# Alternating the two maps' score matmuls of differential attention on the two partition halves, in phases of 512 keys

## What is computed

```python
def diff_attention(q, k, v, lam, lam_init, g_sub, slopes):
    for i in range(S // Q_BLOCK):                       # Q_BLOCK = 128
        kend = q0 + Q_BLOCK
        s = einsum('bqhmd,bkhmd->bhmqk', q[:, q0:kend], k[:, :kend]) * scale
        s = where(allowed, s - slopes * dist, NEG)
        p = softmax(s, axis=-1)
        a = p[:, :, 0] - lam * p[:, :, 1]
        outs.append(einsum('bhqk,bkhe->bqhe', a, v[:, :kend]))
    o = rmsnorm(concatenate(outs, axis=1), g_sub) * (1.0 - lam_init)
```

## Time and profile before

| what | value |
|---|---|
| median of 3 runs | 2858.18 us |
| lowest and highest run | 2855.99 and 2860.78 us |
| span of the profiled execution | 2860.5 us |
| TensorE matmul busy | 2731.5 us, 95% |
| VectorE busy | 1237.1 us, 43% |
| ScalarE busy | 962.7 us, 34% |
| mean granted TensorE clock | 0.961 of full speed |
| share of L1223 (all scores) in the chain that ended last | 5% |

### The profile page before, as it was taken

The page is one execution under the profiler, slowest core; times in us unless marked ns, Lnnn a source line. Parts: engine busy times, 40 slices in busy tenths (PEclk is TensorE's granted clock), DMA queues, the critical chain, the costliest instruction groups (busy, mean ns, idle before and its releaser), DMA issues.

```text
span 2860.5 us, 36998 instructions
## 1 busy us (share of the span) xinstructions
PE 2731.5 (95%) x12825; PEld 2215.9 (77%) x12825; DVE 1237.1 (43%) x2444; ACT 962.7 (34%) x1696; POOL 116.6 (4%) x59
## 2 busy tenths in 40 slices
PE   6999999979999999999989999998899999999998
PEld 5777777768888888888877777776788888888886
DVE  5565664654322322223436666556443222232234
ACT  4344454553321212112334444545423122121223
POOL 3000010001100000000200000000020000000001
PEclk8999998969999999999999999988799999999998
DMA  4100100003111111111130100000211111111112
GB/s 151 30 23 23 29 16 16 16 8 103 44 52 44 51 52 44 51 44 51 44 104 18 28 22 22 16 23 9 74 52 44 52 44 52 44 51 51 44 48 77
DMA packets 214404, 126.40 MB, mean 44 GB/s; under 512 B 14702, under 2 KB 213400, under 8 KB 213528
## 3 DMA queue, kind: packets, MB, share of 16 engines
q1 hardware_dynamic: 214296, 125.09, 14.7%
HBM read 112.49 MB, written 12.58 MB: 44 GB/s over the span
## 4 chain that ended last, share of the span: by engine, by line
PE 85%; DVE 6%; issue 4%; ACT 3%; DVEq 1%; ACTq 0%; DMA 0%; SPq 0%; POOL 0%; POOLq 0%
PE ps L1124 54%; PE ps L1171 18%; PE ps L1223 5%; PE ps L1253 3%; PE ps L1235 2%; PE ps L1255 1%; DVE probs L915 1%; PE ps L1130 1%; ACT probs L615 1%; DVEq L918 1%; PE ps L1193 1%; DVE part L861 1%; PE ps L1365 1%; DVE neg_max L923 1%; DVE part L858 1%
## 5 line engine op out<-in xcount | busy, mean ns | idle before, releaser
L1124 PE MATMUL ps<-h_hi,w_hi 128*128 128x512 f32 x1024 | 315.6, 389 | 0.0
L1124 PE MATMUL ps<-h_lo,w_hi 128*128 128x512 f32 x1024 | 315.3, 389 | 0.0
L1035 DVE TENSOR_TENSOR xt<-ps,xt 128x1024 f32 (+1 forms) x80 | 98.0, 1225 | 502.4 <-PE ps L1124 501.0
L1124 PE MATMUL ps<-u_hi,w_lo 128*128 128x512 f32 x1024 | 315.2, 389 | 0.0
L1124 PE MATMUL ps<-u_hi,w_hi 128*128 128x512 f32 x1024 | 315.2, 389 | 0.0
L1124 PE MATMUL ps<-h_hi,w_lo 128*128 128x512 f32 x1024 | 315.2, 389 | 0.0
L1124 PE MATMUL ps<-u_lo,w_hi 128*128 128x512 f32 x1024 | 315.2, 389 | 0.0
L481 ACT ACTIVATE w_hi<-w_raw 128x1024 fp32r<-128x1024 f32 x144 | 151.2, 1050 | 453.3 <-PE ps L1124 450.7
L1171 PE MATMUL ps<-h_hi,w_hi 128*128 128x512 f32 x736 | 266.7, 444 | 36.1 <-DVE w_lo L846 14.4
L1171 PE MATMUL ps<-h_lo,w_hi 128*128 128x512 f32 x736 | 237.9, 405 | 0.0
L1171 PE MATMUL ps<-h_hi,w_lo 128*128 128x512 f32 x736 | 236.3, 403 | 0.0
(11 more groups left out here) (152 smaller groups left out, 4046.1 us busy)
## 6 DMA issues: line engine op xcount, KB each, us to landing
w_raw<-in_w_up_dram SPq DMA_DIRECT2D x128, 256.0 KB, 3.1
w_raw<-in_w_down_dram SPq DMA_DIRECT2D x128, 256.0 KB, 3.0
w_raw<-in_w_in_dram SPq DMA_DIRECT2D x92, 256.0 KB, 3.2
x_saved<-xt SPq DMA_DIRECT2D x2, 4096.0 KB, 12.9
w_raw<-in_w_out_dram SPq DMA_DIRECT2D x32, 256.0 KB, 3.0
xt<-x_saved SPq DMA_DIRECT2D x4, 2048.0 KB, 7.4
rows<-in_x_dram SPq DMA_DIRECT2D x4, 1024.0 KB, 9.1
out_dram<-rows SPq DMA_DIRECT2D x4, 1024.0 KB, 5.8
```

The lines of the kernel that those rows point to most:

```text
L1035: V.tensor_tensor(xt[:, 2 * m + j], r, xt[:, 2 * m + j], ALU.add).then_inc(evacuated, 1)
L1124: mm = nc.tensor.matmul(ps[j][:, bass.ts(t, BANK)], w[:, j, c], h[:, c, bass.ts(t, BANK)], start=(c == 0 and n == 0), stop=(c == NC - 1 an ...
```

## The change

Both maps' scores of a step are now made together in a phase of up to 512 keys: pass by pass, map 0 on its half of the partitions into bank 0 of `ps[0]`, map 1 on the other half into bank 1. A step of up to 512 keys (i = 0 to 3) has one phase, at the place where map 0's scores stood. A wider step (i = 4 to 7) has a second one for the keys beyond 512, at the place where map 1's scores stood. On VectorE `pair_max` follows the same phases: it reads both banks, writes the maxima of the second phase to a new tile `far_max`, and makes `neg_max` of both maps only after the last phase. The second phase's scores wait until the first has been read. ScalarE's program is unchanged. The number of score passes, their columns and their weight loads are unchanged too.

```diff
--- before.py
+++ after.py
@@ -255,6 +255,7 @@
         eps = small("eps", [P, 1])
         rms_col = small("rms_col", [P, NQ])
         row_max = small("row_max", [P, 8])
+        far_max = small("far_max", [P, 8])
         neg_max = small("neg_max", [P, 8])
         row_sum = small("row_sum", [P, 8])
         sink_exp = small("sink_exp", [P, 8])
@@ -924,6 +925,35 @@
                                             sink[:, bass.ds(sink_at, 1)], neg, ALU.max, ALU.mult)
                     e.then_inc(max_done, 1)
 
+                def pair_max(s0, m0, t, n, key0, width, sc):
+
+                    wide = width > BANK
+                    k1 = min(width, key0 + BANK)
+                    dve.wait_ge(scored, m0 + (n + (1 if wide and key0 == 0 else 2)))
+                    dve.wait_ge(turned, s0 + (t - 1 + CREDIT))
+                    V.memset(wait_slot[:], 0.0)
+                    to = far_max if key0 else row_max
+                    for k in range(2):
+                        at = (n + k) % 8
+                        e = V.tensor_tensor_reduce(out=probs[:, (n + k) % 4, key0:k1],
+                                                   in0=ps[0][:, BANK * k:BANK * k + k1 - key0],
+                                                   in1=far[:, S - width + key0:S - width + k1], scale=1.0, scalar=-3e38,
+                                                   op0=ALU.add, op1=ALU.max, accum_out=to[:, at:at + 1])
+                        if k or not wide:
+                            e.then_inc(scores_read, 1)
+                    if k1 < width:
+                        return
+                    V.drain()
+                    for k in range(2):
+                        at = (n + k) % 8
+                        neg = neg_slope[:, bass.ds(sc + k, 1)]
+                        if wide:
+                            e = V.tensor_scalar(neg_max[:, at:at + 1], row_max[:, at:at + 1], far_max[:, at:at + 1], neg,
+                                                ALU.max, ALU.mult)
+                        else:
+                            e = V.tensor_scalar(neg_max[:, at:at + 1], row_max[:, at:at + 1], neg, None, ALU.mult)
+                        e.then_inc(max_done, 1)
+
                 def combine(m0, n, width):
 
                     dve.wait_ge(exp_done, m0 + (n + 2))
@@ -965,7 +995,8 @@
                             width = window(grp, i)[1] * P
                             n = run.map0[t] + k
                             if grp == "A":
-                                biased_max(s0, m0, t, 1, n, width, far[:, S - width:S], 2 * pair0 + (2 * pp + k))
+                                if k * BANK < width:
+                                    pair_max(s0, m0, t, run.map0[t], k * BANK, width, 2 * pair0 + 2 * pp)
                             elif grp == "B":
                                 at = 2 * (pair0 + pp) + k
                                 biased_max(s0, m0, t, 1, n, width, near[:, 2 * P - width:2 * P], at,
@@ -1225,6 +1256,17 @@
                                                   start=(p == 0), stop=(p == 2))
                     mm.then_inc(scored, 1)
 
+                def pair_scores(m0, n, qs, ks, i, key0, width):
+
+                    k1 = min(width, key0 + BANK)
+                    pe.wait_ge(scores_read, m0 + (n + (1 if key0 else 0) + CREDIT))
+                    for p, (q, k) in enumerate(((q_hi, k_hi), (q_hi, k_lo), (q_lo, k_hi))):
+                        for j in range(2):
+                            half = slice(j * HD, (j + 1) * HD)
+                            mm = nc.tensor.matmul(ps[0][:, BANK * j:BANK * j + k1 - key0], q[half, qs, i * P:(i + 1) * P],
+                                                  k[half, ks, key0:k1], start=(p == 0), stop=(p == 2))
+                    mm.then_inc(scored, 1 if width > BANK else 2)
+
                 def turn_probs(s0, t, slots, b0, blocks, early, ready, count):
                     pe.wait_ge(ready, count)
 
@@ -1268,6 +1310,10 @@
                             pe.wait_ge(split_done, NPART * l + slab0 + (3 if grp == "B" and pp == 2 else 3 * pp - 2))
 
                         n = run.map0[t]
+                        if grp == "A":
+                            if k * BANK < blocks * P:
+                                pair_scores(m0, n, (run.parity + pp) % 2, kv_slot(grp, pp), i, k * BANK, blocks * P)
+                            return
                         p0, read = (BANK * k, n) if grp == "B" else (0, n + k)
                         scores(m0, n + k, (run.parity + pp) % 2, kv_slot(grp, pp), i, k if j is None else j, k0,
                                blocks * P, p0, read)
```

## The result

| what | before | after |
|---|---|---|
| median | 2858.85 us (6 runs) | 2879.96 us (6 runs) |
| lowest and highest run | 2855.99 and 2868.91 | 2870.12 and 2888.83 |
| ratio of after to before, 95% interval | | 1.0072 [1.0056, 1.0088] |
| profiled execution, span | 2860.5 us | 2870.9 us |
| mean granted clock in the profiled execution | 0.961 | 0.957 |

The change costs 21 us. Its direction is that of the forecast and the median lies in its range, near the low end, but the size is half of the 44 us.

What follows compares the result with a forecast made beforehand. TensorE was taken to bound the kernel before, a VectorE-ScalarE chain the wide steps after. The terms summed to +11.0 us a call, +44 for four calls, on 2858.2: 2902 us, 8 in 10 from 2877 to 2932.

Steps and rivals of the forecast that it cites:

- What TensorE saves: Score passes of both maps overlap and narrow steps lose a group each: 65 us if TensorE stayed the bound.
- full overlap at 512 columns: Two maps' score passes of 512 columns on different halves take the time of one; assumed, shown only for 256.
- The chain in the wide steps: Steps 4 to 7: late `neg_max` makes VectorE and ScalarE take turns; 29.4 us, +3.8 and +6.1 in the two heads.
- Steps 0 to 4 of the first head: Narrow steps at a call's start: TensorE's saving less waits for `pt_lo` and the combination, net -2.2 us a call.
- Border and end: Step 7 into the next head, +1.3 us with that head's narrow steps; step 15 to the last turn, +2.0.
- The clock, a rival at 15%: TensorE's clock falls after its new stands, 8 falls costing up to 24 us; result 2905 to 2930; 15%.
- That TensorE stays the bound: Rival: the exponentials catch up and TensorE's saving counts in full, faster by 65 us, 2793; 6%.
- That pairs of 512 don't overlap: Rival: wide score passes gain nothing from pairing, costing 2.4 us a call more, 2912; 9%.
- That the chain costs only what is saved: Rival: each forecast VectorE-ScalarE chain is too long by a fifth; result 2845 to 2875; 12%.
- The rule of the Trainium skill: Row tiling speeds the array but not PSUM evacuation; by that sentence, little or none of the 65 us gain.

Runs made afterwards that it cites:

- x8_first: Kernel before, with both maps' scores paired only in each head's first step (i = 0, 128 keys); 2852.30 us.
- x12_pieces: Changed kernel, with both projection pieces of a wide step put ahead of the values on TensorE, none between second phase and turn; 2877.85 us.
- x1_narrow: Changed kernel, with pairing kept only in steps of up to 512 keys; wider steps go map by map as before; 2833.52 us.
- x14_head0_7: Kernel before, plus pairs in narrow steps and in steps 4 to 6 of a call's first head, those with ScalarE's splits and store ahead of the first exponential; 2828.54 us.
- x5_late_neg: Kernel before, scores map by map; in wide steps only map 0's `neg_max` is made later, after map 1's maximum; 2926.11 us.
- x2_act_order: Changed kernel, with the part's high split and `store_o` moved ahead of the first exponential on ScalarE in wide steps; 2843.94 us.

## Why the forecast was right in sign and wrong in size

**What TensorE saves: right.** The step I was least sure of, full overlap at 512 columns, holds (0.90 us for six passes). The scores' own busy time in layer 0, 288 passes each, before and after:

```profile
95.00:376.00 281.00, 69.05 (x288) 46.22 (x288) 0.98 0.09 23
95.00:384.00 289.00, 40.98 (x288) 23.46 (x288) 0.93 0.08 22
```

That is 28 us less, some 56 in both layers, where the forecast had 65. TensorE's busy time as a whole fell by only 32.6 us, because the values' passes were longer (in layer 0 L1253 and L1255 together 65.0 us before, L1295 and L1297 together 77.2 after) and the turns too. That goes with the lower granted clock of the calls (0.93 against 0.98); how much of it the clock makes isn't separated.

**The chain in the wide steps: right in kind, too long by 1.0 and 1.9 us a stretch.** The forecast's step 5 to 6 was 11.5 us. The changed kernel, VectorE and ScalarE:

```profile
136.44 0.42 DVE L938 CUSTOM_DVE_ANT_0 probs<-ps,far 128x256 f32<-128x256 f32 x1
...
137.31 0.46 DVE L951 TENSOR_SCALAR neg_max<-row_max,far_max,neg_slope 128x1 f32<-128x1 f32 x2
137.62 1.03 ACT L616 ACTIVATE probs<-probs,neg_max,slope_now 128x768 f32<-128x768 f32 x1 [4.79 <-DVE neg_max L951]
...
138.65 1.04 ACT L519 ACTIVATE k_hi<-part 128x1024 fp32r<-128x1024 f32 x1
...
140.19 1.02 ACT L616 ACTIVATE probs<-probs,neg_max,slope_now 128x768 f32<-128x768 f32 x1
...
141.21 1.04 ACT L514 ACTIVATE w_hi<-w_raw 128x1024 fp32r<-128x1024 f32 x1
...
142.28 1.23 DVE L847 TENSOR_TENSOR w_lo<-w_raw,w_hi 128x1024 fp32r<-128x1024 f32 x1 [1.33 <-ACT w_hi L514]
...
143.43 0.68 DVE L901 TENSOR_TENSOR pt_lo<-ps,pt_hi 128x512 fp32r<-128x512 f32 x1
...
144.16 0.38 PE L1295 MATMUL ps<-v_parts,pt_hi 128*128 128x256 f32 x1 [2.68 <-DVE pt_lo L901]
144.23 0.69 DVE L938 CUSTOM_DVE_ANT_0 probs<-ps,far 128x512 f32<-128x512 f32 x1
...
144.84 0.69 DVE L938 CUSTOM_DVE_ANT_0 probs<-ps,far 128x512 f32<-128x512 f32 x1
...
146.04 1.02 DVE L966 SCALAR_TENSOR_TENSOR probs<-probs,lam_ratio 128x768 f32<-128x768 f32 x1
146.98 0.42 DVE L984 TENSOR_REDUCE ps<-ps 128x128 f32<-128x256 f32 x1
147.32 0.55 DVE L938 CUSTOM_DVE_ANT_0 probs<-ps,far 128x384 f32<-128x384 f32 x1
```

Read down, this is the chain of the forecast, link for link, and from 136.44 to 147.32 it takes 10.88 us. From start to start the links are: to the exponential 1.18 (forecast 1.28), two exponentials 2.05 (2.06), `k_hi` and `store_o` 1.54 (1.64), `w_hi` up to `w_lo` 1.07 (1.00), `w_lo` 1.15 (1.15), `pt_lo` 0.80 (0.88), two maxima 1.22 (1.50), up to the combination 0.59 (0.60), combination 0.94 (0.94), reduction 0.34 (0.43). The mis-sized terms are those for which I added durations. Neighbours on one engine start before the one ahead has ended: the two maxima of 512 keys start 0.61 us apart at 0.69 us each, where I had put a gap of 0.07 between them. Step by step the first head has 7.5, 10.9 and 9.1 us (forecast 8.2, 11.5, 9.7). That makes the wide terms 27.5 and 28.4 and not 29.4: 1.9 and 1.0 us a call, 12 of the 28 us by which the sum of the terms (44 us) missed the calls' 15.7.

**Steps 0 to 4 of the first head: the term that failed.** The forecast had -2.2 us, of it 0.7 for step 0; measured is -6.4, which is 17 of the 28 us. I had priced the pair there by TensorE's passes alone and put what the old order cost at a call's start at nothing: a wait of map 1's scores, and the low clock behind it. Rows 1 showed the place, TensorE idle for half of 236 to 242.2, and I put it to the border and took it as given. The timeline of before shows what part of that idle time was:

```profile
236.50 0.33 PE L1223 MATMUL ps<-k_hi,q_hi 64*128 64x128 f32 x1
...
242.27 0.29 DVE L915 CUSTOM_DVE_ANT_0 probs<-ps,far 128x128 f32<-128x128 f32 x1
...
242.63 0.33 PE L1223 MATMUL ps<-k_hi,q_hi 64*128 64x128 f32 x1 [2.75 <-DVE row_max L915]
...
249.00 0.38 PE L1223 MATMUL ps<-k_hi,q_hi 64*128 64x256 f32 x1
```

At the start of the second call, map 1's scores wait 2.75 us for VectorE to read map 0's, with three pieces of projection queued behind them; and the stretch right behind has the low clock, 0.67 in rows 1. After:

```profile
241.76 0.33 PE L1266 MATMUL ps<-k_hi,q_hi 64*128 64x128 f32 x2
...
247.58 0.29 DVE L938 CUSTOM_DVE_ANT_0 probs<-ps,far 128x128 f32<-128x128 f32 x1
...
249.13 0.39 PE L1266 MATMUL ps<-k_hi,q_hi 64*128 64x256 f32 x2
```

Map 1's scores have their own bank and don't wait, so the pieces run meanwhile, and the granted clock of 242.0 to 245.6 us is 1.00. From step 0's scores to step 1's it is 7.4 us instead of 12.5. The fourth call has the same wait (2.76 us before, none after), and in these two calls the whole stretch shrinks by 7.5 us.

The first and third call don't have this wait, before or after, and still shrink by 5.9 and 4.5 us. Their granted clock from the first maximum to step 4 rises from 0.87 and 0.95 to 0.95 and 1.00; in all four calls of before it was below full, in the changed kernel in the first alone. What the score passes bring there and what the clock gives back, no run separates. x8_first, with the pair in step 0 alone, brings 2.6 us of it a call.

**Border and end: right** (a call's step 7 to 12 and its last stretch: +1.0 against +1.3, and +2.4 against +2.0).

**The clock, a rival at 15%: the falls took place, the loss it forecast (2905 to 2930) did not.** Windows of the changed kernel's first call, two stands and the 3.4 us after each:

```profile
140.00:144.40 4.40, 1.72 (x8) 1.10 (x9) 3.07 (x6) 2.90 (x7) 0.00 (x0) 1.00 0.00 0
144.40:147.80 3.40, 3.34 (x18) 2.63 (x18) 3.24 (x10) 0.00 (x0) 0.00 (x0) 0.66 0.57 157
210.00:216.00 6.00, 1.68 (x7) 1.17 (x6) 3.90 (x8) 3.94 (x9) 0.00 (x0) 0.81 0.03 4
216.00:219.40 3.40, 3.40 (x16) 2.75 (x16) 2.78 (x10) 0.00 (x0) 0.00 (x0) 0.50 0.52 147
```

TensorE stands for 2.68 and 4.33 us, and behind it the granted clock is 0.66 and 0.50, the latter the lower of its two levels (1.2 of 2.4 GHz) throughout. The Trainium skill, "TensorE: Matmul & The Clock Gate", section "Part 1: The HAM clock gate (the "warmup" mystery)", has the clock follow how busy the array has been; by that, the trace agrees. The six runs of the change order by it: those with a clock of 0.956 to 0.958 took 2870.12 to 2875.59 us, those with 0.944 to 0.946 took 2884.33 to 2888.83. The profiled execution is one of the first kind, and the 15.7 us of its calls lie below the median's 21. No profile shows where an execution of the second kind has its falls, so that the rest comes from the clock isn't shown. What makes one execution's clock fall oftener stays open: x12_pieces shortened the stands and its runs scattered as much, and so did the kernel before.

What a fall costs depends on what bounds the stretch. Steps 4 to 7 of the changed kernel take 27.47 us at a granted clock of 0.94, and the same stretch in the second call of x12_pieces takes 27.47 at 1.00 (its first call 27.47 at 0.94): nothing, since the chain of VectorE and ScalarE bounds it. Step 7 to 12 takes 40.8 us at 1.00 and 42.4 at 0.96, in x1_narrow and in x14_head0_7. Steps 4 to 7 of x5_late_neg, where TensorE has hardly any slack, take 27.8 at 1.00 and 31.0 at 0.89. So the falls don't make the loss in the changed kernel's steps 4 to 7.

That the median lies inside the forecast's range is in part luck: 2858.85 with the calls' 15.7 us added is 2874.6, below the 2877 at which the range began. The errors of the terms didn't cancel, either: the chain was too long and the start's gain too small, both toward a loss too great.

**The other rivals.** That TensorE stays the bound is out: step 4 to 7 would have come down by more than 3 us from 25.7, and it took 27.5. That pairs of 512 don't overlap is out by the 0.90 us. That the chain costs only what is saved was the nearest miss: the calls' first four steps gave back 6.4 us a call, but the wide steps and the last stretch took 9.2 and the border 1.0. The rule of the Trainium skill, "TensorEngine Tiling (Array Packing)", section "Performance Considerations", that the evacuation of PSUM may become the bottleneck, points at the right side, the engines behind TensorE, but the trace doesn't bear out throughput as the reason. VectorE's work didn't grow (1237.1 and 1235.3 us busy), and x2_act_order got 36 us back by ScalarE's order alone.

## What to carry to other kernels

When a change makes the fast engine's work shorter but hands its result over later, follow who waits for the hand-over in order, and what stands behind the waiting instruction; here one small instruction made late costs 66 us. If the late hand-over can't be avoided, let the waiting engine do the work that doesn't depend on it first: that turned +21 us into -27 with no instruction saved. Pairing only where the hand-over doesn't move did as well here (2833.52 us against 2831.87). Look at the head of each call for waits with a queue behind them before taking an idle stretch as given.

## What the runs showed of the hardware

- Passes on different halves of the partitions, into different banks, overlap fully up to 512 columns: six in 0.90 us, where three on one half took 0.90. Adjacent groups are enough, map by map or alternating: written map by map, the fourth pass of the program still ran beside the first.
- Neighbours on VectorE overlap at their ends: two maxima of 512 keys, 0.69 us each, start 0.61 apart; a combination of 1.02 us is followed after 0.94, a reduction of 0.42 after 0.34. A chain is to be added up from starts.
- Two stands of TensorE, of 2.68 and 4.33 us, were followed by stretches at a granted clock of 0.66 and 0.50. A lower clock went with 2.6 us more in a step of about 10 where TensorE had no idle time (0.79 against 1.00), with 1.6 in a stretch of 41, and with nothing where other engines bound the stretch. The six runs of the change differ by 19 us (2870.12 to 2888.83) and fall into two groups by their granted clock.
